# Halved decay operands in the score levels of a gated linear attention mixer

## The chip, the cores and the metric

One core of one Trainium2 chip runs the whole program. The metric is the device time of one execution in microseconds (us), from the program's start to its end. TensorE is PE, its weight load PEld, VectorE DVE, ScalarE ACT, GpSimd POOL, SyncE SP. Everything is computed in float32 except where noted, for 1024 tokens of width 1024.

## The reference, cut to what matters

The program is one transformer block: an input projection, a gated linear attention mixer ("gla"), a gated delta mixer, an output projection, a routed mixture of 32 experts, and a final part. Only the gla mixer is touched. It has 4 heads with 64 decayed key channels and 128 value channels, in chunks of 64 tokens:

```python
def gla_chunked(q, k, v, log_a):
    causal = jnp.tril(jnp.ones((C, C), bool))[:, :, None]
    def step(S, inp):
        q_c, k_c, v_c, a_c = inp
        b = jnp.cumsum(a_c, axis=-2)
        diff = b[..., :, None, :] - b[..., None, :, :]
        dec = jnp.exp(jnp.where(causal, diff, -jnp.inf))
        attn = jnp.einsum('bhid,bhjd,bhijd->bhij', q_c, k_c, dec)
        o = (jnp.einsum('bhid,bhde->bhie', q_c * jnp.exp(b), S)
             + jnp.einsum('bhij,bhje->bhie', attn, v_c))
```

`attn[i, j]` is a sum over channels of `q_i k_j exp(b_i - b_j)` for j not after i; b falls along a chunk, channel by channel.

## The kernel before, in words

The program runs in stages, each ended by a barrier of all engines: `project` (input projection), `gla`, `delta`, `route`, `experts`, `finish`. `gla(nc, g, sem)` starts at L481. Channels lie on the partitions and the 1024 tokens along the free axis; `p` (0 or 1) names a pair of heads, so that one operand `[128, 1024]` holds a pair.

The decayed scores are built without an array over i, j and channel. `STEPS` (L489) has 14 entries: two for the diagonal and, for each of the levels 0 to 5, one for each pair. At level l the tokens are cut into blocks of 2m with m = 2^l. Scores between a query of the second half of a block and a key of its first half are written as the product of two factors that both stay at or below 1: q times exp(b_i - b_mid) and k times exp(b_mid - b_j), where b_mid is b at the last token of the first half (`v[:, :, m - 1:m]`). The kernel before computes |b - b_mid| for all 1024 tokens, so both halves of Q and K are decayed, and the mask picks the quarter of the block that is wanted.

For a step n of a level, these operations follow each other, in the queue order of each engine as it is written by hand:

- DVE `distance(n)` (L693): `dist[:, n % 2]` = b - b_mid, 128x1024.
- ACT: Abs (L639) and Exp with scale -1/16 (L641) in place.
- DVE `q_level(n)` (L701): Q = q x dist. POOL (L546): K = k x dist. Both 128x1024, both into buffer n % 2.
- PE (L571): 32 matmuls of 128x128 with 64 contracted rows, in four groups that each fill a PSUM bank; steps n and n + 2 share banks.
- DVE `keep(n)` (L709): four masked copies (COPY_PREDICATED) of 128x512 from PSUM into A.

DVE's order is: distance(2), distance(3), then for every n: keep(n), q_level(n + 2), distance(n + 4). POOL clears A, the decayed queries `qe` and the first state S (L537 to L539), then does the k products in order. A q or k product of step n + 2 waits until PE has done the scores of step n (it overwrites their operands); a distance waits for the products of two steps before; the scores of step n wait for both products and for keep(n - 2). DVE waits with its first distance until POOL's three clearings are done (`zeroed`, 3). Buffer 0 of K first holds `reset` (L670 to L672), the 0/1 row with which the running sum b is scanned (L681), two scans for the two pairs.

After keep(13) DVE builds what the chunk states need (L724 to L732), PE transposes the keys (L580), and the states and outputs follow (L592 to L663).

Of the kernel before, what the change touches and what calls it, by code (L numbers as in the profile page):

```python
# [22 lines left out]
ALU = mybir.AluOpType  # L23
ACT = mybir.ActivationFunctionType
AX = mybir.AxisListType

P = 128
T, D = 1024, 1024
# [452 lines left out]
def gla(nc, g, sem):  # L481
# [7 lines left out]
    STEPS = [("diag", p) for p in range(2)] + [(l, p) for l in range(LEVELS) for p in range(2)]  # L489

    with ExitStack() as ph:
        def sb(name, shape, dt=F32):
            return ph.enter_context(nc.sbuf_tensor(name, shape, dt))

        w_gate = sb("w_gla_gate", [16, 2 * P])
        b = sb("gla_b", [P, 2, T])
        A = sb("gla_scores", [P, NH, NT, P])
        dist = sb("gla_dist", [P, 2, T])
        Q = sb("gla_q_level", [P, 2, T])
        K = sb("gla_k_level", [P, 2, T])  # L500
# [9 lines left out]

        wg_in, gv_in, gate_in = sem("w_gate_in"), sem("gv_in"), [sem(f"gate_in{i}") for i in range(2)]
        prep, pre, act_pre, low, logs, run_sum = sem("prepared"), sem("gate_product"), sem("act_softplus"), sem("low"), sem("logs"), sem("running_sum")
        zeroed, dist_done, decay_done, q_done, k_done = sem("zeroed"), sem("distance"), sem("level_decay"), sem("q_level"), sem("k_level")
        score_done, kept = sem("scores"), sem("scores_kept")
        edge_exp, chunk_exp, qe_done, last_dist, kd_done = sem("edge_exp"), sem("chunk_exp"), sem("q_decayed"), sem("last_dist"), sem("k_decayed")
        k_turned, k_natural, added, state_done = sem("k_turned"), sem("k_natural"), sem("state_added"), sem("state_done")
# [5 lines left out]
        def bank_of(step, half, parity):  # L522

            return 4 * (step % 2) + 2 * half + parity

        @block.sync
        def _(sp):
            sp.dma_start(w_gate[:], g.w_gla_gate.rearrange("a k n -> (a k) n")).then_inc(wg_in, 16)
            sp.dma_start(g.gv[:], g.gv_dram.rearrange("(t p) d -> p t d", p=P)).then_inc(gv_in, 16)
            for t in range(NT):  # L530
                if t >= 2:
                    sp.wait_ge(normed, NH * (t - 1))
                sp.dma_start(gate[:, t % 2, :], g.gates_dram[0].rearrange("(t p) d -> t p d", p=P)[t]).then_inc(gate_in[t % 2], 16)

        @block.gpsimd
        def _(pool):
            pool.memset(A[:], 0.0).then_inc(zeroed, 1)  # L537
            pool.memset(qe[:], 0.0).then_inc(zeroed, 1)
            pool.memset(S[:, :, 0, :], 0.0).then_inc(zeroed, 1)  # L539
            for n in range(2, len(STEPS)):  # L540
                level, p = STEPS[n]
                pool.wait_ge(decay_done, n - 1)
                if n >= 4:

                    pool.wait_ge(score_done, 4 * (n - 1))
                pool.tensor_tensor(K[:, n % 2, :], g.gqkT[:, 2 + p, :], dist[:, n % 2, :], ALU.mult).then_inc(k_done, 1)  # L546

        @block.tensor
        def _(pe):
# [75 lines left out]
        @block.scalar  # L625
        def _(act):
            act.wait_ge(prep, 1)
            for p in range(2):
                act.wait_ge(pre, 2 * p + 2)
                src = ps[:, 4 + 2 * p:6 + 2 * p, :].rearrange("p a c -> p (a c)")  # L630
                act.activation(dist[:, p, :], src, ACT.Abs, bias=g.par[:, R_BG + p:R_BG + p + 1]).then_inc(act_pre, 1)
                act.wait_ge(act_pre, 3 * p + 1)
                act.activation(dist[:, p, :], dist[:, p, :], ACT.Exp, scale=-1.0).then_inc(act_pre, 1)
                act.wait_ge(act_pre, 3 * p + 2)
                act.activation(dist[:, p, :], dist[:, p, :], ACT.Ln, bias=one[:, 0:1]).then_inc(act_pre, 1)
                act.wait_ge(act_pre, 3 * p + 3)
            for n in range(2, len(STEPS)):
                act.wait_ge(dist_done, n - 1)
                act.activation(dist[:, n % 2, :], dist[:, n % 2, :], ACT.Abs).then_inc(edge_exp, 1)  # L639
                act.wait_ge(edge_exp, n - 1)  # L640
                act.activation(dist[:, n % 2, :], dist[:, n % 2, :], ACT.Exp, scale=-1.0 / 16).then_inc(decay_done, 1)  # L641

            act.wait_ge(q_done, len(STEPS) - 2)
            act.wait_ge(k_done, len(STEPS) - 2)
            for p in range(2):
                act.activation(dist[:, p, :], b[:, p, :], ACT.Exp, scale=1.0 / 16).then_inc(chunk_exp, 1)
            act.activation(dec[:], b[:].rearrange("p a (c i) -> p a c i", i=C)[:, :, :, C - 1], ACT.Exp, scale=1.0 / 16).then_inc(chunk_exp, 1)
            for p in range(2):
                act.wait_ge(last_dist, p + 1)
                act.activation(Q[:, p, :], Q[:, p, :], ACT.Exp, scale=1.0 / 16).then_inc(chunk_exp, 1)  # L650
            for t in range(NT):
                act.wait_ge(out_done, t + 1)
                for h in range(NH):
                    act.activation(dist[:, 0, h * P:(h + 1) * P], ps[:, 4 + t % 2, h * P:(h + 1) * P], ACT.Square,
                                   accum_out=stat[:, 0, t, h:h + 1]).then_inc(squares, 1)
                act.wait_ge(squares, NH * (t + 1))
                act.activation(stat[:, 1, t, :], stat[:, 0, t, :], ACT.Sqrt, scale=1.0 / P, bias=g.eps[:, 0:1]).then_inc(roots, 1)
                if t >= 1:
                    act.wait_ge(o_turned, t)
                    act.activation(g.mixA[:, :, (t - 1) * P:t * P], ps[:, 6 + (t - 1) % 2, :].rearrange("p (h c) -> p h c", h=NH),  # L660
                                   ACT.Copy, scale=g.par[:, R_GLA:R_GLA + 1]).then_inc(o_kept, 1)
            act.wait_ge(o_turned, NT)
            act.activation(g.mixA[:, :, (NT - 1) * P:T], ps[:, 6 + (NT - 1) % 2, :].rearrange("p (h c) -> p h c", h=NH),  # L663
                           ACT.Copy, scale=g.par[:, R_GLA:R_GLA + 1]).then_inc(o_kept, 1)

        @block.vector
        def _(dve):
# [12 lines left out]
                dve.wait_ge(prep, 3)  # L680
                dve.tensor_tensor_scan(b[:, p, :], reset, Q[:, p, :], 0.0, ALU.mult, ALU.add).then_inc(run_sum, 1)  # L681
            dve.wait_ge(run_sum, 2)
            dve.wait_ge(zeroed, 3)

            def distance(n):
                level, p = STEPS[n]
                m = 1 << level
                v = b[:, p, :].rearrange("p (a i) -> p a i", i=2 * m)
                if n >= 4:

                    dve.wait_ge(q_done, n - 3)
                    dve.wait_ge(k_done, n - 3)
                dve.tensor_tensor(dist[:, n % 2, :].rearrange("p (a i) -> p a i", i=2 * m), v,  # L693
                                  v[:, :, m - 1:m].to_broadcast([P, T // (2 * m), 2 * m]), ALU.subtract).then_inc(dist_done, 1)

            def q_level(n):
                level, p = STEPS[n]
                dve.wait_ge(decay_done, n - 1)
                if n >= 4:
                    dve.wait_ge(score_done, 4 * (n - 1))  # L700
                dve.tensor_tensor(Q[:, n % 2, :], g.gqkT[:, p, :], dist[:, n % 2, :], ALU.mult).then_inc(q_done, 1)  # L701

            def keep(n):
                level, p = STEPS[n]
                mask = g.k[:, K_ID:K_ID + P] if level == "diag" else g.k[:, K_LEVEL + level * P:K_LEVEL + (level + 1) * P]
                for half in range(2):
                    for parity in range(2):
                        dve.wait_ge(score_done, 4 * n + 2 * half + parity + 1)
                        dve.copy_predicated(A[:, 2 * p + parity, 4 * half:4 * half + 4, :],  # L709
                                            mask.bitcast(I32).unsqueeze(1).to_broadcast([P, 4, P]),  # L710
                                            ps[:, bank_of(n, half, parity), :].rearrange("p (t c) -> p t c", t=4)).then_inc(kept, 1)

            distance(2)
            distance(3)
            for n in range(len(STEPS)):
                keep(n)
                if n + 2 < len(STEPS):
                    q_level(n + 2)
                if n + 4 < len(STEPS):
                    distance(n + 4)  # L720
            for p in range(2):
                v = b[:, p, :].rearrange("p (a i) -> p a i", i=C)
                dve.wait_ge(score_done, 4 * len(STEPS))
# [9 lines left out]
            for q in range(4):  # L733
                p, half = q // 2, q % 2
# [1506 lines left out]
```

## Time and profile before

| what | value |
|---|---|
| median of 3 runs | 2805.38 us (2793.61 to 2810.98) |
| the profiled execution, its own time | 2807.38 us |
| its span, first to last instruction | 2805.6 us |
| mean granted TensorE clock | 0.951 |
| busy in the span: PE | 2629.8 us (94%) |
| DVE | 1093.2 us (39%) |
| ACT | 659.4 us (24%) |
| POOL | 251.3 us (9%) |
| the gla stage | about 394 to 567 us |
| its score levels | about 418 to 492 us |

Times in the views are in us from the span's start. A timeline row gives start, length, engine, line, operation, output<-inputs, shape and count; in brackets stands the idle time before it and what ended it. A waits row gives who waited for whom, the total, the number and the longest. The granted clock is the share of TensorE's full speed (1.0 is 2.4 GHz, 0.5 is 1.2 GHz). A row with a count merges neighbours of one kind.

### The profile page before, as it was taken

Reading aid. Unit: us, or ns where it says so; the run is one execution under the profiler, and the core shown is the slowest. Engines: PE = TensorE matmul, PEld = TensorE weight load, DVE = VectorE, ACT = ScalarE, POOL = GpSimd, SP = SyncE. Lnnn points to the kernel's source line nnn. Section 1 sums busy time; section 2 is a strip of 40 time slices with the busy share of each in tenths; the row PEclk is TensorE's granted clock in tenths of the full one; section 3 lists DMA queues with packets and bytes.
Section 4 is the critical chain, followed back from the end, with each engine's and each line's share of the span. In section 5 each row is a group of like instructions: output and inputs, shape, how many; then the busy total and the mean of one; then the engine's idle time right before and its main releaser. Section 6 shows DMA issues by size and latency. Waiting matters only on the chain. (4 is left out here: it accounts for less than half of the span.)

```text
span 2805.6 us, 48229 instructions
## 1 busy us (share of the span) xinstructions
PE 2629.8 (94%) x18983; PEld 2409.6 (86%) x18984; DVE 1093.2 (39%) x1937; ACT 659.4 (24%) x1341; POOL 251.3 (9%) x222
## 2 busy tenths in 40 slices
PE   5999977869989889999999999999999999999798
PEld 4887756649855689999999999999999999999666
DVE  3367629462422352222322323323232323232365
ACT  3224333255311101111111111111111111111245
POOL 0000114035210000000000000000000000000120
PEclk9999976589999789999999999999999999999899
DMA  3111220000053166667888888999999999998541
GB/s 120 54 52 50 86 68 1 23 1 1 16 174 127 62 197 213 222 226 246 257 269 267 274 283 276 304 290 299 291 305 299 302 300 303 301 302 284 201 171 68
DMA packets 439487, 531.87 MB, mean 190 GB/s; under 512 B 12148, under 2 KB 407240, under 8 KB 439368
## 3 DMA queue, kind: packets, MB, share of 16 engines
q1 hardware_dynamic: 425448, 481.08, 52.3%
q0 software_dynamic: 13920, 49.03, 5.6%
q8 instruction: 96, 1.57, 0.2%
q14 instruction: 23, 0.19, 0.0%
HBM read 489.44 MB, written 40.63 MB: 189 GB/s over the span
## 5 line engine op out<-in xcount | busy, mean ns | idle before, releaser
L1590 PE MATMUL ex_psum<-ex_xT,weight_ring_a 128*128 128x134 f32 (+14 forms) x6144 | 768.5, 286 | 0.8 <-ACT ex_xT L1576 0.8
L1590 PEld LDWEIGHTS ex_psum<-ex_xT,weight_ring_a 128*128 128x128 f32 x6144 | 758.7, 191 | 1.2 <-issue 1.2
L1630 PE MATMUL ex_psum<-ex_hT,weight_ring_b 128*128 128x134 f32 (+14 forms) x4096 | 521.5, 286 | 0.0
L1630 PEld LDWEIGHTS ex_psum<-ex_hT,weight_ring_b 128*128 128x128 f32 x4096 | 508.1, 191 | 0.0
L1600 DVE TENSOR_SCALAR ex_gate<-ex_psum,bias_gate_up 128x192 f32<-128x192 f32 x256 | 95.0, 413 | 693.8 <-PE ex_psum L1590 678.5
L1590 PE MATMUL ex_psum<-ex_xT,weight_ring_b 128*128 128x134 f32 (+14 forms) x2048 | 255.6, 286 | 0.0
L1590 PEld LDWEIGHTS ex_psum<-ex_xT,weight_ring_b 128*128 128x128 f32 x2048 | 252.2, 191 | 0.0
L1604 DVE TENSOR_SCALAR ex_up<-ex_psum,bias_gate_up 128x192 f32<-128x192 f32 x256 | 95.0, 413 | 400.9 <-PE ex_psum L1590 400.9
L1617 ACT ACTIVATE ex_sig<-ex_gate 128x384 f32<-128x384 f32 x128 | 66.9, 523 | 718.3 <-DVE ex_gate L1600 718.0
L1638 ACT ACTIVATE ex_yT<-ex_psum,bias_down 128x192 f32<-128x192 f32 x256 | 93.6, 417 | 533.4 <-PE ex_psum L1630 533.4
L1896 PE MATMUL project_psum<-n_hi,w_in_hi 128*128 128x512 f32 x464 | 187.4, 404 | 5.1 <-DVE n_lo L397 5.1
L1458 POOL DMA_INDIRECT ex_rows_a<-xn_dram,ex_list_a x33 | 31.1, 943 | 1728.5 <-DVE ex_list_b L1477 1728.5
L1896 PE MATMUL project_psum<-n_hi,w_in_lo 128*128 128x512 f32 x464 | 182.6, 393 | 0.0
L1896 PE MATMUL project_psum<-n_lo,w_in_hi 128*128 128x512 f32 x464 | 182.4, 393 | 0.0
L1896 PEld LDWEIGHTS project_psum<-n_hi,w_in_hi 128*128 128x128 f32 x464 | 88.2, 190 | 25.3 <-issue 7.6
L1896 PEld LDWEIGHTS project_psum<-n_lo,w_in_hi 128*128 128x128 f32 x464 | 88.1, 190 | 19.8 <-issue 1.9
L1896 PEld LDWEIGHTS project_psum<-n_hi,w_in_lo 128*128 128x128 f32 x464 | 88.1, 190 | 18.9
L1652 PE MATMUL ex_psum<-constants,ex_yT 128*64 128x128 f32 (+1 forms) x528 | 82.0, 278 | 3.4 <-DVE ex_y_a L1659 1.7
L1569 PE MATMUL ex_psum<-constants,ex_rows_a 128*128 128x128 f32 x264 | 64.6, 278 | 10.5 <-issue 9.3
L1617 ACT ACT_TABLE_LOAD x32 | 41.1, 1283 | 138.3 <-DVE ex_gate L1600 138.3
L1612 DVE TENSOR_TENSOR ex_hT<-ex_up,ex_gate 128x384 f32<-128x384 f32 x128 | 71.4, 558 | 4.4
L1608 DVE TENSOR_TENSOR ex_gate<-ex_gate,ex_sig 128x384 f32<-128x384 f32 x128 | 70.6, 552 | 0.9 <-ACT ex_sig L1617 0.9
(320 smaller groups left out, 3070.5 us busy)
## 6 DMA issues: line engine op xcount, KB each, us to landing
weight_ring_a<-in_w_gate_up SPq DMA_DIRECT2D x192, 1024.0 KB, 6.0
weight_ring_b<-in_w_down SPq DMA_DIRECT2D x128, 1024.0 KB, 6.3
weight_ring_b<-in_w_gate_up SPq DMA_DIRECT2D x64, 1024.0 KB, 5.1
y_dram<-ex_y_a SPq DMA_DIRECT2D x33, 512.0 KB, 3.4
w_in_pieces<-in_w_in SPq DMA_DIRECT2D x29, 512.0 KB, 3.2
y_dram<-ex_y_b SPq DMA_DIRECT2D x33, 256.0 KB, 3.7
project_work<-in_x SPq DMA_DIRECT2D x8, 512.0 KB, 3.4
gates_dram<-project_work POOLq DMA_DIRECT2D x16, 256.0 KB, 2.7
```

Of the source, the lines that this page charges most:

```text
L1458: pool.indirect_dma_start(out=rows, out_offset=None, in_=self.g.xn_dram, in_offset=bass.IndirectOffsetOnAxis(ap=index[:, 0:1], axis=0)).th ...
L1569: pe.transpose(into[:, i * CAP:i * CAP + P], self.rows_a[:, k * P:(k + 1) * P], self.ident)
L1590: mm = pe.matmul(self.ps[:, bank, i * CAP:i * CAP + width], w[:, k, i * P:(i + 1) * P], self.xT[:, k, 0:width], start=(k == 0), stop=(k == ...
L1600: dve.tensor_scalar(gate[:, i], self.ps[:, gate_bank, i * CAP:(i + 1) * CAP], bias, 7.0, ALU.add, ALU.min).then_inc(self.gu_kept, 1)
L1604: dve.tensor_scalar(up[:, i], self.ps[:, up_bank, i * CAP:(i + 1) * CAP], bias, -7.0, ALU.add, ALU.max).then_inc(self.gu_kept, 1)
L1608: dve.tensor_tensor(gate, gate, self.sig[:, c % 2], ALU.mult).then_inc(self.act_step, 1)
L1612: dve.tensor_tensor(self.hT[:, 2 * c:2 * c + 2, :], up, gate, ALU.mult).then_inc(self.h_done, 1)
L1617: act.activation(self.sig[:, c % 2], self.gate[:, c % 2], ACT.Sigmoid, scale=1.702).then_inc(self.sig_done, 1)
L1630: mm = pe.matmul(self.ps[:, bank, i * CAP:i * CAP + width], w[:, k, i * P:(i + 1) * P], self.hT[:, k, 0:width], start=(k == 0 and i == 0), ...
L1638: act.activation(self.yT[:, 2 * c + i, :], self.ps[:, self.DOWN[c % 2], i * CAP:(i + 1) * CAP], ACT.Identity, bias=bias).then_inc(self.yT_ ...
L1652: mm = pe.transpose(self.ps[0:n, self.TURN, i * P:(i + 1) * P], self.yT[:, 4 * (q % 2) + i, tokens], self.ident)
L1896: mm = pe.matmul(out, left(k), right(k), start=(k == 0 and n == 0), stop=(k == tiles - 1 and n == 2))
```

## The change

At every level DVE computes only the second half of each block of the distance, as b - b_mid, and POOL the first half, as b_mid - b. Both are at or below zero, so Abs goes and Exp takes scale +1/16. The q product is done for second halves alone and the k product for first halves alone. The other halves of Q and K are cleared once, ahead of the levels, and stay zero. The masked copies and the matmuls are as before.

The clearing of K must come after both scans (K holds `reset`), so POOL waits for the running sum first; its clearings of A, qe and S stand after that and after two k distances. DVE clears Q after its first two distances and then waits for all five clearings. POOL's order in the levels is: k product(n), k distance(n + 2).

```diff
         @block.gpsimd
+            pool.wait_ge(run_sum, 2)
+            pool.memset(K[:], 0.0).then_inc(zeroed, 1)
+            for n in range(2, 4):
+                level, p = STEPS[n]
+                pool.tensor_tensor(halves(dist[:, n % 2, :], level)[0], middle(level, p), halves(b[:, p, :], level)[0], ALU.subtract).then_inc(k_dist, 1)
             pool.memset(A[:], 0.0).then_inc(zeroed, 1)
             pool.memset(qe[:], 0.0).then_inc(zeroed, 1)
             pool.memset(S[:, :, 0, :], 0.0).then_inc(zeroed, 1)
+            def k_distance(n):
+                level, p = STEPS[n]
+                if n >= 4:
+                    pool.wait_ge(q_done, n - 3)
+                    pool.wait_ge(k_done, n - 3)
+                pool.tensor_tensor(halves(dist[:, n % 2, :], level)[0], middle(level, p), halves(b[:, p, :], level)[0], ALU.subtract).then_inc(k_dist, 1)
             for n in range(2, len(STEPS)):
...
-                pool.tensor_tensor(K[:, n % 2, :], g.gqkT[:, 2 + p, :], dist[:, n % 2, :], ALU.mult).then_inc(k_done, 1)
+                pool.tensor_tensor(halves(K[:, n % 2, :], level)[0], halves(g.gqkT[:, 2 + p, :], level)[0], halves(dist[:, n % 2, :], level)[0],
+                                   ALU.mult).then_inc(k_done, 1)
+                if n + 2 < len(STEPS):
+                    k_distance(n + 2)
...
         @block.scalar
-                act.wait_ge(dist_done, n - 1)
-                act.activation(dist[:, n % 2, :], dist[:, n % 2, :], ACT.Abs).then_inc(edge_exp, 1)
-                act.wait_ge(edge_exp, n - 1)
-                act.activation(dist[:, n % 2, :], dist[:, n % 2, :], ACT.Exp, scale=-1.0 / 16).then_inc(decay_done, 1)
+                act.wait_ge(q_dist, n - 1)
+                act.wait_ge(k_dist, n - 1)
+                act.activation(dist[:, n % 2, :], dist[:, n % 2, :], ACT.Exp, scale=1.0 / 16).then_inc(decay_done, 1)
...
         @block.vector
             dve.wait_ge(run_sum, 2)
-            dve.wait_ge(zeroed, 3)
...
-                dve.tensor_tensor(dist[:, n % 2, :].rearrange("p (a i) -> p a i", i=2 * m), v,
-                                  v[:, :, m - 1:m].to_broadcast([P, T // (2 * m), 2 * m]), ALU.subtract).then_inc(dist_done, 1)
+                dve.tensor_tensor(halves(dist[:, n % 2, :], level)[1], halves(b[:, p, :], level)[1], middle(level, p), ALU.subtract).then_inc(q_dist, 1)
...
-                dve.tensor_tensor(Q[:, n % 2, :], g.gqkT[:, p, :], dist[:, n % 2, :], ALU.mult).then_inc(q_done, 1)
+                dve.tensor_tensor(halves(Q[:, n % 2, :], level)[1], halves(g.gqkT[:, p, :], level)[1], halves(dist[:, n % 2, :], level)[1],
+                                  ALU.mult).then_inc(q_done, 1)
...
-            distance(2)
-            distance(3)
+            q_distance(2)
+            q_distance(3)
+            dve.memset(Q[:], 0.0).then_inc(zeroed, 1)
+            dve.wait_ge(zeroed, 5)
```

The two new helpers give the first and second halves of all blocks, and b at each block's middle, repeated:

```python
        def halves(ap, level):
            m = 1 << level
            v = ap.rearrange("p (a i) -> p a i", i=2 * m)
            return v[:, :, 0:m], v[:, :, m:2 * m]

        def middle(level, p):
            m = 1 << level
            return b[:, p, :].rearrange("p (a i) -> p a i", i=2 * m)[:, :, m - 1:m].to_broadcast([P, T // (2 * m), m])
```

## Rows read from the trace of the kernel before

**Rows 1.** Windows, the levels: length, busy PE, PEld, DVE, ACT, POOL, clock, DMA share, GB/s

```profile
418.00:492.00 74.00, 53.21 (x407) 51.60 (x404) 71.35 (x82) 28.70 (x28) 33.35 (x12) 0.68 0.00 1
```

**Rows 2.** Waits, 415 to 487 us: who waited for whom, total, times, longest

```profile
ACT gla_dist L639 <- DVE gla_dist L693: 41.7, 11, 6.3
POOL gla_k_level L546 <- PE gla_psum L571: 25.9, 7, 6.4
```

**Rows 3.** Groups by line, DVE, 418 to 492 us: busy, mean ns, idle before

```profile
L709 DVE COPY_PREDICATED gla_scores<-constants,gla_psum 128x512 f32<-128x512 int32 x56 | 35.8, 721 | 0.0
L701 DVE TENSOR_TENSOR gla_q_level<-gqkT,gla_dist 128x1024 f32<-128x1024 f32 x12 | 20.8, 1731 | 0.0
L693 DVE TENSOR_TENSOR gla_dist<-gla_b 128x1024 f32<-128x1024 f32 x12 | 16.7, 1397 | 2.6 <-POOL gla_k_level L546 2.3
```

**Rows 4.** Timeline of DVE, 398 to 500 us: start, length, line, operation

```profile
415.97 2.29 DVE L681 TENSOR_TENSOR_SCAN gla_b<-gla_k_level,gla_q_level 128x1024 f32<-128x1024 f32 x1
...
420.57 2.54 DVE L709 COPY_PREDICATED gla_scores<-constants,gla_psum 128x512 f32<-128x512 int32 x4
...
432.25 3.31 DVE L701 TENSOR_TENSOR gla_q_level<-gqkT,gla_dist 128x1024 f32<-128x1024 f32 x1
...
440.43 1.22 DVE L693 TENSOR_TENSOR gla_dist<-gla_b 128x1024 f32<-128x1024 f32 x1
441.58 2.58 DVE L709 COPY_PREDICATED gla_scores<-constants,gla_psum 128x512 f32<-128x512 int32 x4
...
491.77 2.34 DVE L724 TENSOR_TENSOR gla_q_level<-gla_b 128x1024 f32<-128x1024 f32 x2
```

**Rows 5.** Timeline of POOL, 394 to 500 us

```profile
394.64 3.51 POOL L537 MEMSET gla_scores<- 128x4096 f32 x1 [5.17 <-POOLq L101]
...
401.54 0.31 POOL L539 MEMSET gla_states<- 128x256 f32 x1
423.12 3.38 POOL L546 TENSOR_TENSOR gla_k_level<-gqkT,gla_dist 128x1024 f32<-128x1024 f32 x1 [21.27 <-ACT gla_dist L641]
...
432.15 2.34 POOL L546 TENSOR_TENSOR gla_k_level<-gqkT,gla_dist 128x1024 f32<-128x1024 f32 x1 [3.34 <-ACT gla_dist L641]
...
440.90 2.99 POOL L546 TENSOR_TENSOR gla_k_level<-gqkT,gla_dist 128x1024 f32<-128x1024 f32 x1 [6.42 <-PE gla_psum L571]
```

**Rows 6.** Timeline of PE, 398 to 500 us, the score matmuls

```profile
426.59 5.01 PE L571 MATMUL gla_psum<-gla_q_level,gla_k_level 64*128 64x128 f32 x32 [5.47 <-POOL gla_k_level L546]
...
452.25 12.58 PE L571 MATMUL gla_psum<-gla_q_level,gla_k_level 64*128 64x128 f32 x96 [4.12 <-DVE gla_q_level L701]
...
483.44 2.82 PE L571 MATMUL gla_psum<-gla_q_level,gla_k_level 64*128 64x128 f32 x32 [0.21 <-DVE gla_q_level L701]
```

**Rows 7.** Windows view, stretches by granted clock (columns as in rows 1)

```profile
445.00:452.00 7.00, 3.13 (x35) 2.82 (x34) 6.97 (x7) 2.12 (x2) 5.56 (x2) 0.99 0.00 0
452.00:462.00 10.00, 9.75 (x65) 9.73 (x65) 9.90 (x14) 4.23 (x4) 3.00 (x1) 0.50 0.01 2
...
483.00:492.00 9.00, 5.87 (x67) 5.29 (x65) 9.00 (x15) 2.15 (x3) 2.36 (x1) 1.00 0.00 1
...
605.00:635.00 30.00, 20.39 (x131) 15.08 (x129) 23.71 (x44) 21.10 (x70) 18.03 (x15) 1.00 0.00 1
```

**Rows 8.** Groups by line and shape, whole run: nearest rows for the halves

```profile
L855 POOL TENSOR_TENSOR dn_state<-dn_state,dn_chunk_decay 128x512 f32<-128x512 f32 x15 | 15.6, 1039 | 62.0 <-DVE dn_state L1145 62.0
...
L828 POOL TENSOR_TENSOR dn_scores_T<-dn_scores_T,constants 128x512 f32<-128x512 f32 x8 | 10.2, 1269 | 36.3 <-DVE dn_scores_T L1104 36.3
...
L1101 DVE TENSOR_TENSOR qkvT<-qkvT,dn_tmp 128x512 f32<-128x512 f32 x8 | 5.5, 682 | 1.8 <-PE dn_psum L861 1.8
...
L670 DVE MEMSET gla_k_level<- 128x1024 f32 x1 | 0.9, 912 | 0.2 <-issue 0.2
```

**Rows 9.** POOL's k product line; DMA queues in 401.8 to 407

```profile
L546 POOLq MODIFY_POOL_CONFIG  x2: 7/9/11, 401.8 to 401.8; - x2
...
q14 instruction: 1, 0.01, 0.5%
```

More of the change, by code:

```diff
@@ L512, in gla @@
         prep, pre, act_pre, low, logs, run_sum = sem("prepared"), sem("gate_product"), sem("act_softplus"), sem("low"), sem("logs"), sem("running_sum")
-        zeroed, dist_done, decay_done, q_done, k_done = sem("zeroed"), sem("distance"), sem("level_decay"), sem("q_level"), sem("k_level")
+        zeroed, decay_done, q_done, k_done = sem("zeroed"), sem("level_decay"), sem("q_level"), sem("k_level")
+        q_dist, k_dist = sem("q_distance"), sem("k_distance")
         score_done, kept = sem("scores"), sem("scores_kept")
@@ L524, in bank_of @@
             return 4 * (step % 2) + 2 * half + parity
+        def halves(ap, level):
+            m = 1 << level
+            v = ap.rearrange("p (a i) -> p a i", i=2 * m)
+            return v[:, :, 0:m], v[:, :, m:2 * m]
+        def middle(level, p):
+            m = 1 << level
+            return b[:, p, :].rearrange("p (a i) -> p a i", i=2 * m)[:, :, m - 1:m].to_broadcast([P, T // (2 * m), m])
         @block.sync
@@ L682, in _, with q_distance @@
             dve.wait_ge(run_sum, 2)
-            dve.wait_ge(zeroed, 3)
-            def distance(n):
+            def q_distance(n):
                 level, p = STEPS[n]
-                m = 1 << level
-                v = b[:, p, :].rearrange("p (a i) -> p a i", i=2 * m)
                 if n >= 4:
@@ L719, in _ @@
                 if n + 4 < len(STEPS):
-                    distance(n + 4)
+                    q_distance(n + 4)
             for p in range(2):
```

## The prediction

> **What bounds the kernel now.** The change touches one stage only, the score levels of the first mixer, so I read that stage's stretch and not the whole. The windows view of it shows 74 us in which DVE is busy 71.35, PE 53.21, POOL 33.35 and ACT 28.70 [rows 1]: DVE is the engine without gaps. The waits of the same stretch say it from the other side: ACT waits 41.7 us in all for DVE's distances and POOL 25.9 us for PE's scores [rows 2], while DVE has 2.6 us of idle time before all of its distances and none before the rest [rows 3]. The groups by line [rows 3] split DVE's time: 56 masked copies, 35.8 us by their recorded lengths; 12 q products with a mean of 1731 ns; 12 distances with a mean of 1397 ns. From the first masked copy at 420.57 to the last step's end at 491.77 [rows 4] are 71.2 us, the piece that the change works on.
>
> The means of the two products hide two lengths. A q product takes about 1.2 us alone and 3.31 at 432.25, where POOL had started its own product 0.10 earlier and runs 2.34 [rows 4, 5]. The other way about, POOL's product at 440.90 takes 2.99 when DVE's distance (440.43, 1.22) is in front of it, while the masked copies at 441.58, which read PSUM, run through it at their usual 2.58 for four [rows 4, 5]. So an elementwise product on DVE with both inputs in SBUF and one on POOL do not overlap here; the masked copy overlaps with either. That is the second constraint after DVE's own length.
>
> **The change, part by part.** Removed: Abs on ACT (12 times). ACT waits 41.7 us in this stretch [rows 2], so this frees nothing by itself.
>
> Halved on DVE: 12 q products and the distances. A DVE operation on 128x512 takes 682 ns [rows 8]; with the start of the next one I take 0.72 us in place of about 1.23. Halved on POOL: 12 k products. Added on POOL: 12 k distances, also halves. POOL's price for 128x512 is 1039 to 1269 ns, where one input is repeated by stride 0 [rows 8], and 2.34 for a whole 128x1024 [rows 5]. The halves here are cut in short runs, down to single elements in the first level, and no row shows POOL on those: the ends are 1.04 (the cheaper form) and 2.34 (no gain from the half). I take 1.27, the nearest row, plus 0.07 to the next.
>
> Moved, and this costs: K must be cleared, but K holds the scan's reset row, so POOL now waits for the running sum. The second scan ends at 415.97 + 2.29 = 418.26 [rows 4]. Before, POOL cleared A, qe and S from 394.64 to 401.85, under other work [rows 5]. Now they stand behind that wait, the clearing of K and two k distances: 418.3 + 1.76 (K, half of the 3.51 of 128x4096) + 2 x 1.34 + 3.51 + 3.51 + 0.31 gives 430.1. DVE's masked copies write A, so the first of them waits there and not at 420.57: 9.5 us later. DVE's own additions, two short distances and the clearing of Q (2 x 0.91 [rows 8]), end at about 421.6, beneath it, whether or not POOL's clearing of K holds the distances back by its 1.76. Queued on POOL behind the clearings is the first k product; on DVE behind the wait is everything.
>
> From 430.1 on I place the instructions one by one: four copies 2.46 (56 of 0.615, start to start, from 2.54 less the tail), a DVE half 0.72, a POOL half 1.34, and 32 score matmuls 5.03 at the granted clock of 0.5 and 2.82 at 1.0 [rows 6, 7]. Copies(0) to 432.6, q(2) to 433.3, scores(2) 433.4 to 438.4 at the low clock. DVE q distance(4) to 434.0; POOL k distance(4) to 435.3 and K(3) to 436.7; copies(1) end at 436.5, so q(3) waits 0.2 and ends at 437.4. Scores(3) 438.4 to 443.4; copies(2) 438.1 to 440.6; q(4) to 441.4; q distance(6) to 442.1; copies(3), held by the last scores, to 444.6; K(5), which needs scores(2) and (3) done, to 444.8; q(5) to 445.5; q distance(7) to 446.2. By then PE has been busy over 10 us. In the trace the clock stood at 0.5 from 452 to 462, with PE busy 9.75 of 10 after a gap, and at 0.99 to 1.0 in the stretches behind such ten busy microseconds [rows 6, 7]; I let it rise in scores(4), which end at 447, copies(4) at 448.7, q(6) at 449.5.
>
> After this the step repeats: q distance 0.72; under the copies (2.46) POOL does one k distance and one k product, 2.67, and the next q product has to wait for them; q 0.72. That is 4.1 us a step, where it was 71.2/14 = 5.1. PE at full clock needs 2.82 and is not the bound. q(12) ends 6 steps later, at 474.1. Copies(11) 2.46, q(13) 0.72, copies(12) 2.46 bring 479.8, and the last scores hold the final copy a little: end at 482.3. Against 491.77 that is 9.5 us gained: about 19 saved in the levels, 9.5 given back in front of them.
>
> One allowance: each step run at the low clock costs 5.03 - 4.1 = 0.93 instead of nothing, at most 6.5 us over seven steps. PE would idle 1.3 of every 4.1. In 605 to 635 it is busy 20.4 of 30 at 1.0 [rows 7], a like share with larger matmuls, so I go near the cheap end and put 2 us. Expected: 7.5 us less. Everything behind is a chain of stages that starts at this stage's end, so it passes on whole. The profiled execution took 2807.4 (span 2805.6 plus 1.8 around it), 2.0 above the median of the runs; 2807.4 - 7.5 = 2799.9 against it, and against the median 2798.
>
> On stride, a rule speaks against the first level. The Trainium skill (Vector Engine (DVE) Microarchitecture Reference, Measured stream behaviour on trn2) says a DVE stream keeps its rate only while it reads or writes at least two adjacent words at a time. In level 0 all three streams take every second word; by its figures, about 2 to 2.5 cycles an element, I estimate 0.6 us more for each of q(2) and q(3), 1 us in the sum at most. No row shows it either way, and the sum leaves it out.
>
> **The rivals.**
> (a) Code loading. Two MODIFY_POOL_CONFIG stand at 401.8 on the line of POOL's first product, which started at 423.12 [rows 5, 9]: whatever they start had 21.3 us to finish unseen. In the new program the first such operation is k distance(2), directly on the path behind the clearing of K at 420.1. The only instruction fetch in 401.8 to 407 is one packet on queue 14 [rows 9]; if the load lasts to about there, the price is up to 5 us: 2.5 gained, 2803 against the median. The rows allow anything from 0 to 21.3; over 7.5 it turns the sign. The Trainium skill (GPSIMD Engine Reference, Instruction dispatch) puts the first call after such a load at about 6 us, unseen in a profile; by it the gain would be 1.5 and the time 2804.
> (b) PE stays at the low clock of 1.2 GHz. Scores are then the pace: 433.4 + 12 x 5.03 + 0.6 = 494.4, 2.6 us later than before: 2808. For it: in the levels the full clock (2.4 GHz) came only after ten busy microseconds and was gone after the gap of 4.12 [rows 6, 7]. Against it: no gap of that length is left.
> (c) The other side: POOL's halves cost as much as whole ones, because of the short runs. Two of 2.34 and gaps, 4.8, stand between q distance and q product, so a step takes 0.72 + 4.8 + 0.72 = 6.2. The first copies start at 432.3, q(2) ends at 435.5, q(12) ten steps later at 497.5, and 8.1 of copies and q(13) end it at 505.6: 13.8 us slower, 2819. It decides from 4.1 + 7.5/10, a step of 4.9, or 1.6 us a half. For it: the short runs. Against: DVE's forms with stride 0 cost nothing extra.
> (d) The change brings no gain because the levels' end is hidden by something else: the k transposes start with the k product after it (L732), and nothing else of the stage stands later. I find no cover.
>
> **How the numbers follow.** Forecast (2798): 0.48. (a) 2803: 0.28. (b) 2808: 0.10. (c) 2819: 0.06. (d) or a clock that falls differently in the later stages, at 0.5 for much of what follows this one: 0.08. All cases lie within 1% of before (28 us, about what a measurement of this kernel can tell from no change), so that is where nearly all chance stands: faster by over 1% 0.02, within 0.96, slower 0.02. The three runs of before lie from 2793.6 to 2811.0, wider than the effect; the range 2788 to 2811 takes in the forecast's best case (no fallback of the clock, 2796, and 8 of scatter), (a), and (b).
>
> **What would show it.** Right: masked copies start at about 430; a step period near 4.1 in the later levels; DVE q products of 0.7 (some longer where POOL is in front); 12 + 12 POOL operations of 1.1 to 1.4; PE's clock mostly 1.0 after 447; the stage's copies done at about 482 to 484. Wrong: a gap of several us on POOL behind the clearing of K (a), PE without gaps at clock 0.5 (b), POOL halves over 1.6 us (c), or copies that start before 428.

## The result and the profile after

The changed kernel takes 2779.3 us by the median of its runs, the kernel before 2796.5 beside it: 17.2 us less by the medians, and a ratio of 0.9933 (95% interval 0.9918 to 0.9949), which is 18.7 us. One of its 19 runs took 15,027 us and stands in neither ratio nor groups. I had forecast 2798 in a range of 2788 to 2811, and 7.5 us of gain. The side was right and so was "within 1%", the size was not, and the time lies below the range. A second, later set of runs gave 0.9952 (0.9931 to 0.9972), 13.4 us less.

The profiled execution of the changed kernel took 2777.5 us (span 2775.8). Against the one of before that is 29.8 us, far more than either ratio says, so this pair of profiles holds something that most pairs of runs don't. The time by part, from the timelines and the stage barriers:

| part | before | after | difference |
|---|---|---|---|
| up to the end of the second scan | 418.26 | 417.56 | -0.7 |
| levels: end of scan to the last masked copy | 73.5 | 61.0 | -12.5 |
| behind the levels, to the stage's end (567.5, 539.0) | 75.7 | 60.5 | -15.2 |
| all later stages | 2238.1 | 2236.8 | -1.3 |

First the levels. POOL's timeline of the changed kernel (columns as in [rows 5]):

```profile
417.62 1.80 POOL L551 MEMSET gla_k_level<- 128x2048 f32 x1 [27.59 <-DVE gla_b L709]
419.47 2.03 POOL L554 TENSOR_TENSOR gla_dist<-gla_b 128x512 f32<-128x512 f32 x2
421.45 3.50 POOL L555 MEMSET gla_scores<- 128x4096 f32 x1
...
428.36 0.30 POOL L557 MEMSET gla_states<- 128x256 f32 x1
428.63 1.49 POOL L572 TENSOR_TENSOR gla_k_level<-gqkT,gla_dist 128x512 f32<-128x512 f32 x1
...
447.07 1.55 POOL L564 TENSOR_TENSOR gla_dist<-gla_b 128x512 f32<-128x512 f32 x1 [0.98 <-DVE gla_q_level L725]
448.58 1.27 POOL L572 TENSOR_TENSOR gla_k_level<-gqkT,gla_dist 128x512 f32<-128x512 f32 x1
```

The chain in front of the levels is the one I had laid out: clearing of K, two k distances, the three clearings. A k distance takes 1.03 alone (2.03 for two) where I had 1.27; in the levels its row says 1.55 (447.07), because it starts 0.04 behind DVE's short distance (447.03 to 447.72) and has to let it pass. The first one starts 0.05 behind the clearing of K, in spite of the MODIFY_POOL_CONFIG that stands there at 419.4 now: no load is waited for. DVE answers (columns as in [rows 4]):

```profile
417.59 1.29 DVE L718 TENSOR_TENSOR gla_dist<-gla_b 128x512 f32<-128x512 f32 x2
...
428.69 2.56 DVE L734 COPY_PREDICATED gla_scores<-constants,gla_psum 128x512 f32<-128x512 int32 x4 [7.66 <-POOL gla_states L557]
431.15 0.67 DVE L725 TENSOR_TENSOR gla_q_level<-gqkT,gla_dist 128x512 f32<-128x512 f32 x1
...
446.32 0.67 DVE L725 TENSOR_TENSOR gla_q_level<-gqkT,gla_dist 128x512 f32<-128x512 f32 x1
447.03 0.69 DVE L718 TENSOR_TENSOR gla_dist<-gla_b 128x512 f32<-128x512 f32 x1
447.64 2.55 DVE L734 COPY_PREDICATED gla_scores<-constants,gla_psum 128x512 f32<-128x512 int32 x4
450.09 0.67 DVE L725 TENSOR_TENSOR gla_q_level<-gqkT,gla_dist 128x512 f32<-128x512 f32 x1
...
478.52 2.33 DVE L751 TENSOR_TENSOR gla_q_level<-gla_b 128x1024 f32<-128x1024 f32 x2
```

DVE waits 7.66 us for POOL's last clearing, then runs without a gap: from one q product to the next are 3.77 us (446.32 to 450.09). The two distances at 417.59 take 1.29 together under POOL's clearing of K, no more than such halves take elsewhere (0.69 each by their records, which overlap a little), so a POOL operation that only writes does not hold back a DVE one with two inputs. Level 0 reads and writes every second word and its q product at 431.15 costs 0.67 like the others: the penalty for such a stream that the Trainium skill gives (Vector Engine (DVE) Microarchitecture Reference, Measured stream behaviour on trn2) is not there. The groups by line, 418 to 479 us (columns as in [rows 3]):

```profile
L734 DVE COPY_PREDICATED gla_scores<-constants,gla_psum 128x512 f32<-128x512 int32 x56 | 35.8, 719 | 7.7 <-POOL gla_states L557 7.7
L725 DVE TENSOR_TENSOR gla_q_level<-gqkT,gla_dist 128x512 f32<-128x512 f32 x12 | 9.1, 761 | 0.0
L718 DVE TENSOR_TENSOR gla_dist<-gla_b 128x512 f32<-128x512 f32 x12 | 8.2, 692 | 0.4
```

The q products fell from 20.8 to 9.1 us: about half of it is the length, the rest is that only one of them (1.71) still stands behind a POOL product, where before three q products and one distance took 3.3. PE has 2.82 per step and about 0.95 idle:

```profile
447.05 2.82 PE L600 MATMUL gla_psum<-gla_q_level,gla_k_level 64*128 64x128 f32 x32 [0.95 <-DVE gla_q_level L725]
```

Then the part that I had passed over. The windows view, of the kernel after and below it of the one before (columns as in [rows 1]):

```profile
440.00:478.00 38.00, 27.66 (x319) 25.74 (x316) 37.76 (x61) 10.61 (x11) 23.27 (x17) 1.00 0.01 1
479.00:513.00 34.00, 26.00 (x190) 20.21 (x190) 21.95 (x47) 5.97 (x20) 0.00 (x0) 0.51 0.03 9
514.00:537.00 23.00, 20.64 (x163) 13.69 (x164) 8.50 (x33) 12.07 (x60) 0.00 (x0) 1.00 0.20 58
```

```profile
493.00:567.00 74.00, 63.91 (x360) 44.04 (x360) 30.35 (x81) 19.61 (x83) 0.00 (x0) 0.50 0.08 22
```

In both kernels TensorE drops to 0.5 (1.2 GHz) in the idle stretch behind the last scores. After the change it was back at 1.0 (2.4 GHz) at 514, in the middle of the outputs; before, it stayed at 0.5 to the end of the stage. The outputs hang on it. (The reciprocal below is one operation of each tile's output.) One tile of them follows the other in DVE's timeline by 3.55 us at 1.0 (after) and by 6.16 at 0.5 (before):

```profile
524.91 0.18 DVE L773 RECIPROCAL gla_stat<-gla_stat 128x4 f32<-128x4 f32 x1 [2.20 <-ACT gla_stat L685]
...
528.46 0.18 DVE L773 RECIPROCAL gla_stat<-gla_stat 128x4 f32<-128x4 f32 x1 [2.20 <-ACT gla_stat L685]
```

```profile
551.23 0.18 DVE L746 RECIPROCAL gla_stat<-gla_stat 128x4 f32<-128x4 f32 x1 [4.82 <-ACT gla_stat L657]
...
557.39 0.18 DVE L746 RECIPROCAL gla_stat<-gla_stat 128x4 f32<-128x4 f32 x1 [4.82 <-ACT gla_stat L657]
```

The change touches no instruction of that part. So the questions for the runs: what of the gain is the change's own, and does the clock behind the levels belong to it?

### The profile page after: what moved, and what is told of

It reads as the page before. It is cut to its first block and busy times, and to the rows that moved or that the text cites. A ratio compares the mean times of both kernels' runs of the same rounds, so it can differ in the third digit from the quotient of the medians.

```text
span 2775.8 us, 48252 instructions
## 1 busy us (share of the span) xinstructions
PE 2598.6 (94%) x18983; PEld 2384.0 (86%) x18984; DVE 1074.1 (39%) x1938; ACT 646.5 (23%) x1329; POOL 252.9 (9%) x235
```

## The experiments

**The kernel before, again** (no edit).

> The kernel before, unchanged, for a second profile and for the clock of each timed run. Theory A (two lengths of the output part): the runs fall into two groups about 11 to 15 us apart (near 2794 and near 2806), the longer ones with the lower mean granted clock, and a profile of the shorter group shows the stage's part behind the levels at 60 to 65 us with TensorE's clock back at 1.0 inside it, where the first profile has 75.7 us at 0.5. Theory B (the profile of before was one odd execution): all runs near 2794 to 2800, clock of each the same within 0.001. The levels take 73.5 us from the end of the second scan to the last masked copy under both.

Its levels took 76.0 us, and the part behind them 65.8: the clock came back for its last 17 us.

```profile
493.00:541.00 48.00, 39.19 (x251) 28.45 (x251) 25.88 (x61) 10.86 (x42) 0.00 (x0) 0.54 0.06 17
541.00:558.00 17.00, 14.36 (x112) 9.50 (x110) 6.03 (x24) 8.31 (x42) 0.00 (x0) 0.99 0.18 47
```

The 25 runs of the kernel before on that chip fall into 6 from 2790.9 to 2798.3 with a mean clock of 0.953 to 0.958 and 19 from 2802.5 to 2813.0 with 0.949 to 0.953; the 12 runs of this experiment into 2 and 10. Theory A holds: this program has two lengths, and the profile on which I predicted was of the longer one. The 2.5 us more in the levels are one more q product behind POOL (23.3 us for the twelve, where [rows 3] has 20.8), which I had not expected.

**Early clearings** in the changed kernel.

```diff
         def _(pool):
+            pool.memset(A[:], 0.0).then_inc(zeroed, 1)
+            pool.memset(qe[:], 0.0).then_inc(zeroed, 1)
+            pool.memset(S[:, :, 0, :], 0.0).then_inc(zeroed, 1)
             pool.wait_ge(run_sum, 2)
             pool.memset(K[:], 0.0).then_inc(zeroed, 1)
...
-            pool.memset(A[:], 0.0).then_inc(zeroed, 1)
-            pool.memset(qe[:], 0.0).then_inc(zeroed, 1)
-            pool.memset(S[:, :, 0, :], 0.0).then_inc(zeroed, 1)
```

> The changed kernel with the clearings of A, qe and S put back ahead of the wait for the running sum, where the kernel before has them; the clearing of K and the two k distances stay behind it. Theory A (they are on the path of the changed kernel): the first masked copy starts at about 421.5 in place of 428.7 and the levels end 7.2 us sooner, near 471.3; the time falls by 7, to about 2772. Rival (the first scores are held by something else, PE at its low clock after the gap, for instance): the first copy starts early but scores of steps 2 and 3 at the low clock pace the levels, and less than 4 us are left of it. Neither says which clock the output part gets.

The first masked copy starts at 420.29, 7.6 us sooner from the scan's end, and the levels take 55.2 us, 5.7 less. So the moved clearings are on the path and cost about six. The 1.9 us that are missing are in two places. The first q product now meets POOL's k product and takes 1.57 in place of 0.67 (DVE's timeline, the first view below). And the clock fell at 465: the last scores took 8.17 for two steps instead of 5.64 (PE's timeline, the second view), of which 1.0 us reached the last masked copy:

```profile
422.74 1.57 DVE L725 TENSOR_TENSOR gla_q_level<-gqkT,gla_dist 128x512 f32<-128x512 f32 x1
```

```profile
463.20 8.17 PE L600 MATMUL gla_psum<-gla_q_level,gla_k_level 64*128 64x128 f32 x64 [2.00 <-DVE gla_q_level L725]
```

The time was 2773.7, ratio to before 0.9902 (0.9869 to 0.9935).

**Late clearings** in the kernel before: the same three lines behind a new `pool.wait_ge(run_sum, 2)`, and DVE's `wait_ge(zeroed, 3)` behind `distance(3)`.

> The kernel before with one part of the change alone: the clearings of A, qe and S stand behind the wait for the running sum, and DVE waits for them after its first two distances. Theory A: the first masked copy starts at 418.3 + 7.3 = 425.6 in place of 420.6, the whole of the levels shifts by 5.0 us, nothing else changes, and the time rises by 5. Rival: POOL's first products come later too but DVE's stalls behind POOL (3 to 5 of 2 us each) fall differently, and the levels' end shifts by 2 or less.

The first copy is at 424.90, 5.0 us later from the scan's end as expected, but the levels take 74.5 us, between the 73.5 and 76.0 of the two profiles without the edit; ratio 1.0006 (0.9985 to 1.0028). The rival was right. DVE's 2.31 us of waiting for POOL and the first blocked distance, 3.29 long, are gone, because POOL's first k product now runs under the masked copies: the twelve distances take 14.6 us in place of 16.7. The ratio alone could not tell 0 from 5 us; by the groups of runs the edit costs 0.2 us in the shorter one and 1.7 in the longer. A delay of 5 us ahead of DVE was thus worth 0 to 2 us in this kernel, since it took stalls away; in the changed kernel, whose DVE has no such stalls to lose, 5.7 of 7.6 us count.

**Products only**: halves for the q and k products; distances, Abs and Exp on all tokens as before; early clearings.

```diff
-                pool.tensor_tensor(K[:, n % 2, :], g.gqkT[:, 2 + p, :], dist[:, n % 2, :], ALU.mult).then_inc(k_done, 1)
+                pool.tensor_tensor(halves(K[:, n % 2, :], level)[0], halves(g.gqkT[:, 2 + p, :], level)[0], halves(dist[:, n % 2, :], level)[0],
+                                   ALU.mult).then_inc(k_done, 1)
```

> The halved q and k products alone: distance, Abs and Exp as before on all 1024 tokens, on DVE and ACT; clearings of A, qe, S early, of K behind the scans, of Q on DVE. Theory A (DVE's own work is the bound): a step is four copies 2.45, half a q product 0.70, a whole distance 1.23 less the overlap at the copies, about 4.3 us where the change has 3.77 and the kernel before 5.1 on average; the levels end near 421.0 + 13.5 x 4.3 = 479. Rival (most of the change's gain in a step comes from POOL no longer blocking DVE): the blocked DVE products of 3.3 us are gone already here and a step is 3.8 to 4.0.

The levels took 67.9 us, so neither number was right: the mean step is 4.7. Half of the q products still stand behind POOL, which waits for the same thing as they do (Exp), and take 1.7 to 1.9:

```profile
449.33 1.67 DVE L711 TENSOR_TENSOR gla_q_level<-gqkT,gla_dist 128x512 f32<-128x512 f32 x1
```

Of the 18 to 21 us between the kernel before (73.5 to 76.0) and the one with early clearings (55.2), halving the products gives 6 to 8, and moving half of the distance from DVE to POOL gives 12.7. With the second part goes Abs too, and the first copy starts 1.1 us sooner; no run takes Abs away alone, so its share in the 12.7 is not known. The second part is the larger, and it removes the collisions: POOL then works right behind DVE's short distance, under the masked copies.

**Added matmuls.** The next seven runs ask what the clock behind the levels is worth, with matmuls that nothing reads, n0 of them in PE's idle gap and n1 behind each state product (in the runs a helper with the numbers put in):

```diff
+            pe.wait_ge(kept, 4 * len(STEPS))
+            for _ in range(n0):
+                pe.matmul(ps[:, 7, 0:P], g.gqkT[:, 0, 0:P], g.gqkT[:, 1, 0:P], start=True, stop=True)
...
                 mm.then_inc(added, 1)
+                for _ in range(n1):
+                    pe.matmul(ps[:, 7, 0:P], g.gqkT[:, 0, 0:P], g.gqkT[:, 1, 0:P], start=True, stop=True)
```

With n0 = 44 and n1 = 4, on three kernels:

> The kernel before, with matmuls added whose results nothing reads (128x128x128 into the last PSUM bank): 44 between the last masked copies and the key transposes, where PE sits idle for about 8 us, and 4 behind each of the 15 state products. Theory A (behind the levels the time hangs on TensorE's clock, which falls in that idle gap and does not come back): the clock stays at 1.0 from the levels' end to the stage's end, the part behind the levels takes about 56 us in place of 75.7 (or 65.8 in the second profile), all runs lie in one group near 2787, and the mean clock is 0.960 or more. Rival (the low clock there is only a companion, the ACT and DVE steps of the outputs set the pace): the added matmuls cost their own time or nothing, the part stays at 65 to 76 us and the two groups remain. The levels are untouched: 73.5 to 76 us.

> The changed kernel with the same added matmuls. Theory A: the part behind the levels takes about 56 us in every run (60.5 in the profile of the changed kernel without them), one group of runs near 2774. Against the kernel before with the same additions the difference is then that of the levels alone, 12.5 to 15 us. Rival (the change has a second effect of its own behind the levels): the difference between the two kernels with added matmuls is 18 us or more, or under 10.

> The changed kernel with the clearings of A, qe and S put back ahead of the wait, and the added matmuls. Theory A: the parts add, levels 55 us and the part behind them 56: about 2768, 5 to 7 us under the changed kernel with added matmuls, one group of runs. Rival: the clock falls inside the levels (it did at 465 in the run without added matmuls) and stays low for ten microseconds, and 3 or less of the gain is left.

The clock did what theory A says. From the changed kernel's profile:

```profile
477.00:515.00 38.00, 36.59 (x342) 32.09 (x343) 21.05 (x43) 2.12 (x2) 0.00 (x0) 1.00 0.01 1
515.00:548.00 33.00, 29.09 (x228) 19.18 (x226) 10.44 (x40) 17.39 (x81) 0.00 (x0) 1.00 0.17 49
```

From the third tile on the outputs now ran at 3.54 us a tile, in the kernel before as in the changed one. But I had mis-sized the additions: one such matmul is 0.23 us, so 44 took 10.09, and four behind a state product took 1.16 where DVE's pace is 0.70 for the whole. The part behind the levels came to 72 us in both, some 16 of them my own by the 56 expected. What the pair shows is the difference between the kernels with the clock held in both profiled executions: 73.9 against 61.0 us in the levels and nothing behind them. The medians are 2804.5 and 2788.1, 16.4 apart, between what theory A (12.5 to 15) and its rival (18 or more) wanted, and 3.5 more than the levels; that rest is not explained. Nor did the longer runs vanish: 3 of 12 of the kernel before stand at 2815 to 2821 and 2 of 12 of the changed one at 2809, with lower mean clocks. With early clearings the median is 2781.3, all 6 runs within 6 us.

Then n0 = 24 with n1 = 0, and n0 = 24 with n1 = 1 on three kernels:

> The changed kernel with 24 added matmuls (results unread, 24 x 0.23 = 5.5 us, as the 88 records of 44 took 10.09 us in the runs before) in PE's idle gap behind the last masked copies, and none among the state products. Theory A (the clock falls in that gap): it stays at 1.0 through the state products and the outputs, the part behind the levels takes 56 us, one group of runs at about 2773. Rival (the state products, small and paced by DVE at 0.70 us each, let the clock fall by themselves): the clock is at 0.5 again before the outputs start, the part takes 60 to 76 us and runs fall into two groups as without additions.

> The same with one more added matmul behind each of the 15 state products (0.27 each, of which 0.15 to 0.2 beyond DVE's pace of 0.70, 3 us in all). Theory A: clock at 1.0 throughout the part, 59 us in every run, one group near 2776. Rival: one added matmul in 0.85 us is too little, the clock falls among the state products, and the two groups stay, 3 us later each.

> The kernel before with the same additions (24 in the gap, one behind each state product). Theory A: the part behind the levels takes 59 us here too, where it was 75.7 and 65.8 in two profiles; the runs gather near 2789, and the difference to the changed kernel with the same additions is that of the levels, 12.5 to 15 us. Rival: part of the difference between the kernels is neither levels nor clock, and it comes out at 17 or more.

> The changed kernel with the clearings of A, qe and S put back ahead of the wait, and the same additions. If both parts add: levels 55 us, the part behind them 59, about 2770, and no group of longer runs; it would be the shortest by its median. Rival: the early clearings alone (2773.7 in 6 runs) are as good, since the additions cost what the clock gives back.

The rivals won. The gap was filled; the clock fell to 0.5 at 479.4 all the same, stood at 1.0 from 482.8 to 489.6, and was gone when the state products came:

```profile
483.00:489.00 6.00, 4.52 (x39) 4.04 (x38) 5.94 (x7) 0.00 (x0) 0.00 (x0) 1.00 0.00 0
490.00:553.00 63.00, 59.98 (x344) 40.92 (x344) 19.66 (x71) 17.49 (x81) 0.00 (x0) 0.50 0.09 25
```

Medians: 2792.0 with the gap filled alone, 8 of 12 runs between 2790 and 2795 and 4 between 2778 and 2780; 2799.6, 2818.4 and 2799.5 with one more behind each state product (changed, before, early clearings). Each is longer than that of the same kernel without additions, since at 0.5 a state product and its addition took 1.77 us where I had reckoned 0.85. The 18.8 us between the first two would fit the rival, but they hold unlike groups: group by group the kernels are 12.5 and 15.8 apart, for 14.9 in the levels of their profiles (75.9 and 61.0). Holding the clock this way does not pay. What kind of work would raise it at less cost stays open.

**The changed kernel again, the early clearings again, and a delay**: seven clearings of Q on DVE behind the last masked copies, each with a wait for the one before.

> The changed kernel, unchanged, again. Theory A (the change itself, or how its levels end, makes a run of the longer group rarer): again about one run in four or fewer lies near 2793 and the rest near 2778; the kernel before beside it has about two in three in its longer group (2802 and more). Rival (the groups are drawn alike for every kernel with this part behind the levels, and 4 of 18 was chance): about two in three of the runs lie near 2793, and the median difference to the kernel before shrinks to the 13 to 15 us of the levels.

> The changed kernel with the clearings of A, qe and S put back ahead of the wait, again, for its median beside that of the changed kernel on one chip. Levels 55.2 us again, 5.7 us less than the changed kernel's 61.0; group by group 5 to 7 us under it (near 2772 and 2786). Rival (its levels end with the clock at 0.5, which in the first profile lengthened the last two scores): more runs in the longer group than the changed kernel has, and a median no better.

> The changed kernel with seven clearings of Q (1.76 each, 12.7 us in all, results unread) on DVE between the last masked copies and what follows: the levels' end then stands where it stood before the change, and PE is idle 12.7 us longer. If saved time in the levels passes whole to the end: each group 12.7 us later, near 2791 and 2806. Theory A (which group a run falls into depends on how PE was used before the outputs): the longer idle time of PE makes the longer group more frequent, two in three as in the kernel before. Rival (no such dependence): the share of the longer group is that of the changed kernel beside it.

Changed kernel: 6 runs from 2778.6 to 2784.8 (clock 0.960 to 0.962) and 6 from 2789.7 to 2794.8 (0.955 to 0.959); its profile is of the latter, levels 61.0, the clock at 0.5 from 480.8 to beyond the stage's end, and 75.7 behind the levels, as in the kernel before. The kernel before had 11 of 23 in its longer group there. So in this set the shares are alike, and with the first set (4 of 18 against 9 of 19) they are 10 of 30 against 20 of 42. That the change makes the longer group rarer is not shown by these; the profiles after with 60.5 and 75.7 us show that it has both. It is not excluded either: on the chip of the first four experiments, beside 29 longer runs of 37 of the kernel before, early clearings had 1 of 6 and products only 2 of 8, while late clearings, which leave the kernel's whole products, had 9 of 12. And with the gap filled alone the shares were alike again (8 of 12 against 22 of 35 of the kernel before).

The delay was 15.8 us, not 12.7 (each wait adds 0.49), and its groups lie at 2795.4 (8 runs) and 2808.9 (4 runs), 15.3 and 16.7 above those of the changed kernel (2780.1 and 2792.2): time saved in the levels does pass whole to the end. The longer idle time of PE did not make the longer group more frequent (4 of 12, beside 6 of 12 without the delay), against theory A. What decides a run's group is left open.

Early clearings: 2775.4, ratio 0.9922 (0.9893 to 0.9951), levels 55.3. Over both sets its lower group is at 2768.8 to 2776.3 (9 of 12 runs), 5 to 7 us under the changed kernel's. It beats both kernels, with the edit shown above.

## Why the prediction was wrong

By the groups of runs, the change gives 15.7 us in the shorter one (2794.3 to 2778.6) and 12.3 in the longer (2805.4 to 2793.1) in the first set, 14.0 and 14.6 in the second. That is what the levels show: 73.5 to 76.0 before, 61.0 after in each of five profiles. The whole ratio moves between 13 and 19 us with how many runs of each group a set holds.

Term by term against my sum:

- The structure held: DVE is the bound, the masked copies do not shrink, the moved clearings delay the first copy. Its start, 11.8 us behind the scan's end in my sum, was 11.1. That Abs is worth nothing by itself was not tested.
- **The step that failed first is "POOL's half takes 1.27, so a step is 4.1".** A k distance takes 1.03. It repeats one element in a row, as the cheaper of my two rows does (L855, 1039), while the dearer (L828, 1269) repeats a whole 128x128 mask [rows 8]; I took them as one form. Counted from the end of DVE's short distance, 1.03 and the product's 1.27 fit under the copies with 0.24 to spare, so no q product waits (my sum had 0.2 of waiting a step), and DVE's distance takes 0.61 to the next start where I had 0.72. A step is DVE's own 3.77. From the first copy to the end that was 2.4 us less than in my sum.
- **The clock allowance of 2 us was not needed.** The clock was at 1.0 from 438.8 to 479.8 with PE idle a quarter of each step. The row at 605 to 635 [rows 7] had said so. The rise after "ten busy microseconds" was a misreading too: here it came 6.9 us behind the first scores (431.87), and in the kernel before the clock was also at 1.0 from 431.5 to 434.9, behind 5.0 us of scores [rows 6].
- The start (0.7), the steps (2.4) and the clock (2.0) make the 7.5 us into 12.6. The rest of 14 is in the reference: I took the levels of before at the 73.5 of one profile; two of the four profiles of kernels with its levels have one blocked product more (75.9 and 76.0).
- **The range failed at "the profiled execution ... 2.0 above the median of the runs".** I read the runs 2793.6, 2805.4, 2811.0 as scatter about one median. They were one of a group near 2794 and two of a group near 2806, and the profile was of the upper one. The measured 2796.5 for the same kernel is 8.9 lower than my anchor, as much as the whole gain I forecast. A row that I had could have warned me, with TensorE at 0.50 from 492 to 585 and PE busy 69.8 of these 93 us; I wrote of it only as a residual case. The row stands below this list.
- "Everything behind passes on whole" is right, by the delay run.

The windows view of the kernel before (columns as in [rows 1]):

```profile
492.00:585.00 93.00, 69.82 (x374) 47.74 (x375) 35.10 (x96) 26.98 (x97) 0.52 (x1) 0.50 0.07 18
```

The rivals: code loading is refuted, 0.07 us from MODIFY_POOL_CONFIG to the first operation. PE at the low clock: the first scores ran at it until 438.8, yet the steps there took 3.79 to 3.81, so it cost nothing; at the levels' end with early clearings it cost 1 us. POOL halves as dear as whole ones: no, 1.03 and 1.27 where nothing is in front; short runs cost a little, 1.49 to 1.52 for the k products of levels 0 and 1 against 1.27 from level 2 on.

## What to carry to other kernels

Before anchoring a forecast on a profile, put its mean clock and time beside the other runs: a few runs 12 us apart may be two lengths of one program, and then a median of three is a coin toss. Where two engines exclude each other, as here, look not only at how long each works but at what releases them together: give the second its work right behind the first one's short piece and under something that does not collide. And when an operand must be prepared later, move only that one: the three clearings had no reason to move with it, and cost 5.7 us.

## What the runs showed of the hardware

- A POOL operation that only writes SBUF (clearing of K) and a DVE operation with two SBUF inputs overlapped freely; POOL products and DVE products never did. The Trainium skill (SBUF — State Buffer, Who interferes with whom) states just this, and the trace agrees: two half distances take 1.29 us together beside the clearing, and a whole one 3.29 behind a product, where it takes 1.22 alone.
- After MODIFY_POOL_CONFIG the first POOL product followed in 0.07 us; the some 6 us that the Trainium skill (GPSIMD Engine Reference, Instruction dispatch) gives for a first call behind it did not appear.
- TensorE at 0.5 did not rise in 63 us with PE busy 60 of them (state products and outputs, gap filled alone), and rose in other executions in the same work, 35 to 48 us behind the levels' end. In the profiles with four more 128x128 matmuls behind each state product it stayed at 1.0 from before the state products to the stage's end. What decides it is open.
